# Value products of the prompt attention: from four bursts a head to three, the last four units at the next head's first step

## What is computed

```python
def fox_attend(q, k, v, cq, ck, q_pos, k_pos):
    s = jnp.einsum("bqhd,bkhd->bhqk", q, k, preferred_element_type=jnp.float32) * (HEAD_DIM ** -0.5)
    bias = jnp.swapaxes(cq, 1, 2)[:, :, :, None] - jnp.swapaxes(ck, 1, 2)[:, :, None, :]
    mask = k_pos[None, :] <= q_pos[:, None]
    p = jax.nn.softmax(jnp.where(mask, s + bias, -jnp.inf), axis=-1)
    return jnp.einsum("bhqk,bkhd->bqhd", p.astype(v.dtype), v)

def sb_attend(q, k, v, q_pos, k_pos):
    z = jnp.einsum("bqhd,bkhd->bhqk", q, k, preferred_element_type=jnp.float32) * (HEAD_DIM ** -0.5)
    mask = k_pos[None, :] < q_pos[:, None]
    log_1m = jnp.where(mask, jax.nn.log_sigmoid(-z), 0.0)
    suffix = lax.cumsum(log_1m, axis=3, reverse=True) - log_1m
    a = jnp.where(mask, jnp.exp(jax.nn.log_sigmoid(z) + suffix), 0.0)
    return jnp.einsum("bhqk,bkhd->bqhd", a.astype(v.dtype), v)
```

## Time and profile before

| | |
|---|---|
| median of 3 runs | 1053.74 us (1053.7 to 1054.9) |
| the profiled execution | 1052.99 us, its span 1051.2 us |
| PE, DVE, ACT, POOL busy | 1006.0, 664.0, 463.5, 281.7 us |
| PE in the chain that ended last | 77% |
| granted TensorE clock, mean | 0.996 of full |
| forgetting heads, from about 652 to 799 us | some 17 us a head |
| stick-breaking heads, from about 799 to 989 us | some 23 us a head |

### The profile page before, as it was taken

The page is one execution under the profiler, slowest core; times in us unless marked ns, Lnnn a source line. Parts: engine busy times, 40 slices in busy tenths (PEclk is TensorE's granted clock), DMA queues, the critical chain, the costliest instruction groups (busy, mean ns, idle before and its releaser), DMA issues.

```text
span 1051.2 us, 27360 instructions
## 1 busy us (share of the span) xinstructions
PE 1006.0 (96%) x11220; PEld 855.6 (81%) x11220; DVE 664.0 (63%) x982; ACT 463.5 (44%) x912; POOL 281.7 (27%) x293
## 2 busy tenths in 40 slices
PE   6899999999999999999999998999988999999997
PEld 5898778987778898987889887888876888887786
DVE  5658355644676346756557631777778887787387
ACT  5522302221132222232313322767798887887353
POOL 2300000000000001111011110341187566666497
PEclk9999999999999999999999999999999999999999
DMA  6367697688889787788888796875544442521443
GB/s 231 112 241 238 216 328 299 260 354 321 318 332 322 304 310 289 297 316 300 320 309 322 296 291 187 241 171 122 134 99 102 97 101 62 108 62 51 141 160 141
DMA packets 121474, 234.02 MB, mean 223 GB/s; under 512 B 60553, under 2 KB 91273, under 8 KB 103953
## 3 DMA queue, kind: packets, MB, share of 16 engines
q1 hardware_dynamic: 96016, 209.33, 59.0%
q10 hardware_dynamic: 25344, 23.08, 6.4%
HBM read 204.52 MB, written 27.86 MB: 221 GB/s over the span
## 4 chain that ended last, share of the span: by engine, by line
PE 77%; DVE 7%; POOL 5%; issue 5%; ACT 4%; DMA 2%; ACTq 1%; DVEq 0%; POOLq 0%; SPq 0%
PE bank L890 29%; PE bank L877 8%; PE bank L954 7%; PE bank L1000 6%; PE bank L1743 5%; PE bank L1250 5%; PE bank L1226 4%; PE bank L1203 4%; PE bank L983 3%; DVE pr L1487 2%; PE bank L1265 1%; PE bank L1181 1%; DVE om L1498 1%; POOL o_nat L1918 1%; DMA k_buf<-in_cache_sb_k 1%
## 5 line engine op out<-in xcount | busy, mean ns | idle before, releaser
L890 PE MATMUL bank<-w_hi,hT_hi 128*128 128x256 f32 (+1 forms) x896 | 260.1, 290 | 3.2 <-DVE hT_lo L623 2.5
L890 PE MATMUL bank<-w_lo,hT_hi 128*128 128x256 f32 (+1 forms) x896 | 253.1, 283 | 0.0
L890 PE MATMUL bank<-w_hi,hT_lo 128*128 128x256 f32 (+1 forms) x896 | 252.9, 282 | 0.0
L890 PEld LDWEIGHTS bank<-w_hi,hT_hi 128*128 128x128 f32 x896 | 170.6, 190 | 10.3 <-DVE hT_lo L623 5.5
L890 PEld LDWEIGHTS bank<-w_lo,hT_hi 128*128 128x128 f32 x896 | 170.9, 191 | 0.3 <-issue 0.2
L890 PEld LDWEIGHTS bank<-w_hi,hT_lo 128*128 128x128 f32 x896 | 170.6, 190 | 0.0
L537 ACT ACTIVATE u_out<-bank 128x256 f32<-128x256 f32 x112 | 42.9, 383 | 273.4 <-PE bank L890 273.0
L733 DVE STREAM_TRANSPOSE k_buf<-k_buf 128x2048 f32<-128x2048 f32 x64 | 145.3, 2291 | 5.8 <-DMA k_buf<-in_cache_sb_k 5.5
L1608 POOL TENSOR_TENSOR pr<-pr,om 128x1023 f32<-128x1023 f32 (+3 forms) x64 | 94.5, 1483 | 65.4 <-DVE om L1498 49.2
L1226 PE MATMUL bank<-ident,pr 128*128 128x128 f32 x576 | 86.9, 278 | 5.1 <-POOL pr L1608 2.6
L1250 PE MATMUL bank<-pT,v_nat 128*64 128x128 f32 x1152 | 85.6, 280 | 0.0
(11 more groups left out here) (217 smaller groups left out, 1950.0 us busy)
## 6 DMA issues: line engine op xcount, KB each, us to landing
k_buf<-in_cache_fox_k SPq DMA_DIRECT2D x32, 1024.0 KB, 9.5
v_ring<-in_cache_fox_v SPq DMA_DIRECT2D x32, 1024.0 KB, 7.8
k_buf<-in_cache_sb_k SPq DMA_DIRECT2D x32, 1024.0 KB, 8.9
v_ring<-in_cache_sb_v SPq DMA_DIRECT2D x32, 1024.0 KB, 7.4
w_raw<-in_w_in SPq DMA_DIRECT2D x14, 1024.0 KB, 9.4
out<-u_out ACTq DMA_DIRECT2D x72, 128.0 KB, 5.2
q_scratch<-u_out ACTq DMA_DIRECT2D x64, 128.0 KB, 5.5
k_nat<-out SPq DMA_DIRECT2D x32, 256.0 KB, 4.1
```

What stands on the lines that cost most here:

```text
L890: mm = pe.matmul(bank[:, U + i % 2, w_cols(c)], a[:, k, hcols(s)], b[c % 2][:, k, w_cols(c)], start=(k == 0 and n == 0), stop=(k == KD - 1 ...
```

## The change

The tuple of units is changed for two steps. At step 0 the value products of four units are issued, units 4 to 7 of the head before (back 4, 3, 2, 1), where there were two (back 2, 1). At step 6 none are issued, except in the last head, which has no next head and keeps its two. Steps 2 and 4 are as before. So each of the fifteen handovers from one head to the next has the seven products of units 4 and 5 in another place, two steps later, and a head has three bursts instead of four. No product, no buffer and no other engine's program is changed.

```diff
                     transpose_p(p, hh, u, g)
-                    for back in (1,) if turning else (2, 1) if u % 2 == 0 else ():
+                    whole = (4, 3, 2, 1) if u == 0 else () if u == 6 and following else (2, 1)
+                    for back in (1,) if turning else whole if u % 2 == 0 else ():
                         if u:
                             outputs(p, hh, u - back, g)
                         elif hh:
```

## The result

Eight executions of the changed kernel have a median of 1063.09 us, eight of the kernel before 1054.93 us. The ratio on record is 1.0067 with an interval of 1.0049 to 1.0084: slower by 7.1 us (5.2 to 8.9); the two medians alone differ by 8.2. The profiled execution took 1063.22 us, its span 1061.5.

A forecast was written before the change was run, and what follows sets the result against it. PE carries 77% of the chain, but DVE's waits end last at step 6, so freed time counts nothing; added bursts less gaps cost 2.7 us in forgetting heads and their end plus 2.7 in the others, 5.4: 1059.1 us, range 1054.5 to 1062.5.

The forecast's parts named there:

- The freed time is worth nothing: Step 6, heads 0 to 14: PE free 1.08 us earlier per head, all idle behind DVE's row maxima or `yaT_lo`.
- The added burst, 0.76: Step 0, heads 1 to 15: 14 more records at 0.054 each add 0.76 us; bounds zero and 1.02.
- the signs: Trace signs expected after, among them a step 0 burst of 19 or 20 value-product records, near 1.35 us.
- Cover in forgetting heads: Gaps behind the burst, heads 1 to 7: 0.28 or about 0.2 us, more at some heads, all covered into head 7.
- Cover in stick-breaking heads, 0.37: Step 2, heads 10 to 14: PE's 0.37 us wait for ACT absorbs part of 0.76, leaving 0.39 each, 1.95 together.
- The handover into head 8, 0.3 with a bound of 1.0: Change of attention kind, granted clock 0.50: added burst costs 0.3 us at full clock, up to 1.0 at half.
- ACT's `oT` hides with 0.5 to spare: Stick-breaking step 0: ACT reaches the accumulator's move at 895.96, the products' successor would start at 895.4; no cost.
- The rule of the Trainium skill: Value-product bursts at step 6 and step 0: tiling-mode changes drain TensorE, so one burst fewer saves; alone 4.8 us gain.
- PE is the pace: Rival, step 7 projection and step 0 scores: each removed burst returns 1.08 for 0.76, 4.8 us faster, 1048.9; 9%.
- The burst sinks into gaps: Rival: PE's new idle at step 7 is handed on, waits absorb the step 0 burst; 1053.7 to 1055 us; 11%.
- The idle time costs the clock: Rival, stick-breaking heads: about 1 us more idle lowers the clock in three heads, 4.5 us on top, about 1063.6; 4%.
- HAM oscillation: Skill's warning that idle gaps between groups of matmuls bring the clock down; taken as speaking against the change.

The follow-up runs named there:

- without the products: Changed kernel with units 4 and 5 issued neither at step 6 nor step 0 (handovers into heads 2 to 15); 1057.41 us, 1.0024 of before.
- the products at both places: Changed kernel with units 4 and 5 computed at step 6 as well as in the step 0 burst; 1064.01 us, 1.0085 of before.

## Why the prediction was right, and which sizes were off

The forecast was 1059.1 us, 5.4 more than the median shown; the change costs 7.1 by the timed executions and 8.1 by distances. On the forecast's scale that is 1053.74 times 1.0067, 1060.8 us, inside its 1054.5 to 1062.5; the measured median, 1063.09, belongs to executions in which before had 1054.93. The direction and the mechanism held; three sizes did not.

- **The freed time is worth nothing: right.** It was priced at 1.08 us a head and counted as idle behind `yaT_lo` and the row maxima. The trace of after has just these waits (1.00 us; 0.34 and 0.59), and the runs without the products and with them at both places show it by effect: some 14 us of PE's work taken away there, and some 15 added, change no distance of a middle stick-breaking head by more than 0.02.
- **The added burst, 0.76: it was 0.87.** The step that failed is the price of 0.054 a record, read between the bursts of 14 and 30 records. The 22 records of the merged burst (not 19 or 20 in 1.35 us, as the signs had it) take 1.46 us, as by that line; but the 8 of the short burst had taken only 0.59, from the row below to 894.64, and the step from 8 to 14 records costs 0.43, 0.072 a record. The line was right where I had rows and was used outside them, though the short burst was in the trace.

```profile
894.05 0.54 PE L1250 MATMUL bank<-pT,v_nat 128*64 128x128 f32 x5
```

- **Cover in forgetting heads: right.** The burst of 0.87 less the measured distances gives covers of 0.30, 0.41, 0.20, 0.64, 0.20 and 0.86 behind the handovers into heads 1 to 6; taken were 0.28, 0.28, 0.2, 0.51, 0.2 and 0.66, and into head 7 all is covered as foreseen (the wait of 1.53 us has become 0.65). The sum of these seven handovers is 2.6 against 2.4.
- **Cover in stick-breaking heads, 0.37: it was 0.17.** ACT's wait at step 2 did go (906.11 above). But PE then arrives earlier at step 4, where DVE's `k_hl` had ended only 0.16 us before PE's turn of `oT` (880.64 and 880.80 in before, below), and waits 0.24 there: `k_hl` ends 9.0 us behind the `none` record in both kernels. A covered wait was counted as a gain without a look at the next one on the way. Four heads cost 0.70 each instead of 0.39: 2.8 against 1.6. Into head 9, with no gap, 0.87 against 0.76; into heads 14 and 15 together 0.37 against 0.39, which may be luck, since 14 to 15 differs by 0.25 between kernels alike.

```profile
879.95 0.69 DVE L1477 TENSOR_TENSOR k_hl<-bank,k_hl 64x512 fp32r<-64x512 f32 x1
...
880.80 0.66 PE L1265 MATMUL bank<-ident,oT 128*128 128x128 f32 x4
```

- **The handover into head 8, 0.3 with a bound of 1.0: it was 1.5**, and 2.4 with the products at both places. The bound took the half clock for the 14 added records alone, less the wait of 0.5 behind them. In after the half level lasts 6.8 us instead of before's 3.4 and takes in the eight transposes ahead of the burst as well: 0.9 us more for these and 1.4 for the burst (2.43 against 1.05 to the next scores), of which only a part comes back behind it. Why it lasted longer is not shown. Together: 2.6 + 1.5 + 0.9 + 2.8 + 0.4 = 8.2, the 8.1 of the distances.
- **ACT's `oT` hides with 0.5 to spare: right.** Where the earlier trace rows had it 1.3 us behind PE's next scores, it now starts 0.45 behind them:

```profile
904.44 0.63 ACT L1403 ACTIVATE oT<-bank 128x512 f32<-128x512 f32 x1
```

- **The rivals.** *PE is the pace* is refuted by the run without the products. One burst fewer saves PE 0.2 us a head, 1.08 removed for 0.87 added, but the saving lies on the idle side, so it returns nothing. The rule of the Trainium skill, "TensorEngine Tiling (Array Packing)", Tiling Modes, would make a burst fewer cheaper, and the rows agree in direction; that the change of mode is what the 0.2 us pay for, no run here shows. *The burst sinks into gaps* holds at heads 6, 7 and 15 and nowhere else. *The idle time costs the clock* did not come true in the seven stick-breaking heads with a new wait of about 1 us: the granted clock stays at 1.00 there (891 to 915 us above, and 1.00 in the mean of 808 to 1000). At the change of kind the half level lasts longer than in before; but it does so with the products at both places too, where the waits ahead of it are before's, so that the added idle time is the cause is not shown. The Trainium skill, "TensorE: Matmul & The Clock Gate", HAM oscillation, warns of idle gaps between groups of matmuls; the trace agrees with it at the change of kind, in before as in after, and new waits of 1.0 us a head brought no half level.

## What to carry to other kernels

Work on the busiest engine is free where another engine's result is waited for anyway and costs its full price where none is, so moving it out of such a place was a loss here even though it saved a burst. Before a covered wait is counted as a gain, look for the next semaphore on the same engine: here 0.37 us of cover were worth 0.17, since `k_hl` was tied 0.16 behind. And where a stage ahead varies by several microseconds from execution to execution, compare the distances of one repeated record: they settle tenths of a microsecond that medians can't.

## What was not expected of the hardware

But for 14 to 15 and the change of kind, distances between heads whose program is the same agree to 0.03 us between kernels, on two chips, while the start of the prompt moved by some 7 us (649.2 to 656.0) in ten profiled executions, and the stretch behind the last burst took 62.1 to 62.2 us in each.

At the change of kind the half clock does not fall on the same work in each kernel. The eight transposes of head 8's unit 0, without and with the half level, in the kernel without the change at that place and in that without the products:

```profile
801.10 1.09 PE L1226 MATMUL bank<-ident,pr 128*128 128x128 f32 x8 [2.25 <-POOL pr L1611]
```

```profile
801.09 1.97 PE L1226 MATMUL bank<-ident,pr 128*128 128x128 f32 x8 [1.76 <-POOL pr L1610]
```

The second had waited 1.68 us for ACT just before, the first 0.51. But the kernel with the products at both places waited 0.51 and has 1.97 as well, so what decides it stays open. Where the burst is before's, the time is given back within the head: from these transposes to the `none` record into head 9, 26.98 us in the kernel without the products against 26.96 in before. Only with the long burst in it is it paid, in after and with the products at both places.
